# Compressed attention: the upper four token tiles take their exponential without bias and without sum

## The reference, cut to what matters

```python
def compressed_attention(q, k_cmp, v_cmp, pos, slopes):
    end_idx = np.arange(n_cmp) * CMP_STRIDE + CMP_BLOCK - 1
    s = jnp.einsum('bghtd,bgcd->bghtc', q, k_cmp).astype(jnp.float32) * NSA_HEAD_DIM ** -0.5
    dist = (pos[:, :, None] - pos[:, end_idx][:, None, :]).astype(jnp.float32)
    valid = np.arange(S)[:, None] >= end_idx[None, :]
    s = s - slopes[None, :, :, None, None] * dist[:, None, None]
    s = jnp.where(valid, s, NEG_INF)
    m = jnp.max(s, axis=-1, keepdims=True)
    p = jnp.where(valid, jnp.exp(s - m), 0.0)
    p = p / jnp.maximum(jnp.sum(p, axis=-1, keepdims=True), 1e-20)
    o = jnp.einsum('bghtc,bgcd->bghtd', p.astype(v_cmp.dtype), v_cmp)
    return o, p
```

## Time and profile before

| what | value |
|---|---|
| median of 3 runs | 2379.27 us (2377.95 to 2382.49) |
| profiled execution | 2378.9 us, span in the profile 2377.1 us |
| busy over the span | PE 89%, DVE 40%, ACT 30%, POOL 20% |
| the stage | from 1329 us to the barrier, next matmul at 1416.75 us |

### The profile page before, as it was taken

How to read it: one execution, slowest core, us unless ns; L and a number is a source line. 1 busy time by engine, 2 the same in 40 slices (tenths; PEclk the granted TensorE clock), 3 DMA queues, 4 the chain that set the end, 5 groups by cost and what they waited for, 6 DMA issues and landing times. The chain is left out here.

```text
span 2377.1 us, 32726 instructions
## 1 busy us (share of the span) xinstructions
PE 2119.5 (89%) x12669; PEld 1469.5 (62%) x12669; DVE 960.4 (40%) x2286; ACT 717.8 (30%) x1775; POOL 474.0 (20%) x617
## 2 busy tenths in 40 slices
PE   6997759999899999967999648999999999999995
PEld 3444336655688888843654525666665568888883
DVE  3997864532512111113123576666662242111111
ACT  3014455511111111130121656676662111111110
POOL 0001003321112222100000334454441001222211
PEclk9998769999899999989999779999999998999998
DMA  5000011031779999954000100001002147999995
GB/s 204 0 0 0 0 62 37 19 101 71 298 270 358 366 368 368 325 171 106 0 1 0 74 1 10 11 20 45 10 10 74 62 173 275 360 366 370 369 349 137
DMA packets 88034, 347.27 MB, mean 146 GB/s; under 512 B 16721, under 2 KB 21864, under 8 KB 70919
## 3 DMA queue, kind: packets, MB, share of 16 engines
q1 hardware_dynamic: 69446, 278.03, 30.4%
q0 software_dynamic: 18432, 67.12, 10.9%
HBM read 288.84 MB, written 60.47 MB: 147 GB/s over the span
## 5 line engine op out<-in xcount | busy, mean ns | idle before, releaser
L1530 PEld LDWEIGHTS experts_gu_ps<-experts_x_cols,moew_gate 128*128 128x128 f32 x2048 | 242.3, 195 | 34.3 <-issue 34.3
L1530 PE MATMUL experts_gu_ps<-experts_x_cols,moew_gate 128*128 128x128 f32 x2048 | 243.2, 278 | 4.6 <-DVE experts_x_cols L1567 4.6
L1530 PE MATMUL experts_gu_ps<-experts_x_cols,moew_up 128*128 128x128 f32 x2048 | 239.1, 275 | 0.0
L1530 PEld LDWEIGHTS experts_gu_ps<-experts_x_cols,moew_up 128*128 128x128 f32 x2048 | 233.8, 192 | 0.0
L1541 PE MATMUL experts_y_ps<-moew_down,experts_hid 128*128 128x512 f32 x512 | 230.5, 593 | 2.0 <-DVE trunk_x_rows L1623 2.0
L1070 POOL TENSOR_SCALAR nsaatt_probs<-nsaatt_probs,nsaatt_inv,trunk_gates_or_logits 128x384 f32<-128x384 f32 (+7 forms) x256 | 181.6, 726 | 209.3 <-DVE nsaatt_inv L1095 209.3
L1616 DVE TENSOR_TENSOR experts_sig<-experts_gu_ps,experts_sig 128x256 f32<-128x256 f32 x64 | 27.2, 425 | 440.3 <-ACT experts_sig L1579 440.3
L1041 ACT ACTIVATE nsaatt_probs<-nsaatt_probs,nsaatt_bias 128x384 f32<-128x384 f32 (+7 forms) x256 | 169.0, 667 | 17.7 <-DVE nsaatt_bias L1090 17.7
L1470 POOL DMA_INDIRECT x_kept<-trunk_x_rows,moe_index x64 | 101.4, 1585 | 308.0 <-DVE trunk_x_rows L1623 214.0
L1541 PEld LDWEIGHTS experts_y_ps<-moew_down,experts_hid 128*128 128x128 f32 x512 | 92.5, 191 | 95.4 <-issue 95.4
L1579 ACT ACTIVATE experts_sig<-experts_gu_ps 128x256 f32<-128x256 f32 x64 | 24.7, 386 | 416.6 <-PE experts_gu_ps L1530 416.6
(11 more groups left out here) (377 smaller groups left out, 3229.1 us busy)
## 6 DMA issues: line engine op xcount, KB each, us to landing
moew_gate<-in_moe_w_gate_dram SPq DMA_DIRECT2D x64, 1024.0 KB, 7.5
moew_up<-in_moe_w_up_dram SPq DMA_DIRECT2D x64, 1024.0 KB, 11.8
moew_down<-in_moe_w_down_dram SPq DMA_DIRECT2D x64, 1024.0 KB, 15.1
trunk_x_rows<-in_x_dram SPq DMA_DIRECT2D x16, 512.0 KB, 4.7
x_kept<-trunk_x_rows SPq DMA_DIRECT2D x16, 512.0 KB, 2.6
h_rows<-out_h_rows SPq DMA_DIRECT2D x16, 512.0 KB, 2.6
trunk_x_rows<-x_kept SPq DMA_DIRECT2D x16, 512.0 KB, 4.1
l0b_w_in<-in_mix_w_in_dram SPq DMA_DIRECT2D x1, 5760.0 KB, 23.7
```

The source lines that it names most:

```text
L1530: last = pe.matmul(to, wm[:, c, half * P:(half + 1) * P], x_cols[:, s % 2, c, :], start=(c == 0), stop=(c == CHUNKS - 1))
```

## The change

For the upper four tiles (`BY_ROW` = 4 to 7) the exponential takes neither a bias nor a sum. DVE subtracts the row's maximum in `e` itself, in one instruction of 4 tiles by 2 heads by 63 keys (504 elements), placed in `shift(i)` between the maximum and the bias. ACT then takes four tiles of one head in one activation of 252 elements, so a pair has two such activations and eight of the old kind, ten in place of sixteen (`EXPS`). The sums of the upper tiles are a reduction of 504 elements at the head of `normalise(i)` on DVE. It waits only for the two wide activations, which ACT takes first. `shifted` now counts two for a pair, and ACT waits for both.

```diff
+    BY_ROW = TILES // 2
+    EXPS = 2 * BY_ROW + 2
+    REST = (P, TILES - BY_ROW, 2, W)
...
                 def exps(i):
-                    act.wait_ge(shifted, i + 1)
+                    act.wait_ge(shifted, 2 * (i + 1))
                     if i >= 2:
                         act.wait_ge(p_ready, i - 1)
-                    for t in range(TILES):
+                    for h in range(2):
+                        rows = e[:, i % 2, BY_ROW:, h, 0:W]
+                        act.activation(rows, rows, ACT.Exp, scale=SLOPES[2 * i + h]).then_inc(exped, 1)
+                    for t in range(BY_ROW):
                         for h in range(2):
                             act.activation(e[:, i % 2, t, h, 0:W], ... bias=..., accum_out=...).then_inc(exped, 1)
...
                     mine.link(dve.tensor_reduce(top[:, :, :], rows, X_AXIS, ALU.max))
+                    dve.tensor_tensor(rows[:, BY_ROW:], rows[:, BY_ROW:], over(top[:, BY_ROW:, :].unsqueeze(3), REST),
+                                      ALU.subtract).then_inc(shifted, 1)
                     if i >= 2:
-                        dve.wait_ge(exped, 2 * TILES * (i - 1))
-                    dve.tensor_tensor(bias[:, b], top[:, :, :], over(slopes[:, 2 * i:2 * i + 2, 1].unsqueeze(1), (P, TILES, 2)),
-                                      ALU.mult).then_inc(shifted, 1)
+                        dve.wait_ge(exped, EXPS * (i - 1))
+                    dve.tensor_tensor(bias[:, b, 0:BY_ROW], top[:, 0:BY_ROW, :],
+                                      over(slopes[:, 2 * i:2 * i + 2, 1].unsqueeze(1), (P, BY_ROW, 2)), ALU.mult).then_inc(shifted, 1)
...
                 def normalise(i):
...
-                    dve.wait_ge(exped, 2 * TILES * (i + 1))
+                    dve.wait_ge(exped, EXPS * i + 2)
+                    dve.tensor_reduce(total[:, b, BY_ROW:, :], rows[:, BY_ROW:], X_AXIS, ALU.add).then_inc(rest_summed, 1)
+                    dve.wait_ge(exped, EXPS * (i + 1))
+                    dve.wait_ge(rest_summed, i + 1)
```

More of the change, by code:

```diff
@@ L2348, in compressed @@
                                 "added", "turned", "copied", "valued", "out_ready"))
-        gates_ready = ph.sem("gates_ready")
+        gates_ready, rest_summed = ph.sem("gates_ready"), ph.sem("rest_summed")
         with nc.Block() as block:
```

## The result

The changed kernel takes 2385.53 us (median of 10 runs, 2384.39 to 2390.57), the kernel before 2379.93 us in the same series (10 runs, 2377.5 to 2382.49): 5.6 us more. Over all the runs, not from the two medians, the ratio is 1.0026 with a 95% interval of 1.0016 to 1.0036. It is slower, by a little more than a measurement of this kernel can tell from no change. The forecast was 2385.1 us, from a median before of 2379.27; its sum was 5.9 us more.

The account below looks back on a forecast made before the run. The prediction took a DVE-POOL loop of 6.82 us a turn, not ACT, as the bound. Start -1.13, turns +6.55 and end +0.5 gave +5.9 us, predicted 2385.1 us, range 2381.9 to 2387.4 (8 in 10).

Parts of the forecast that it names:

- What bounds the stage: Stage of the change: DVE's waits for POOL's product close each 6.82 us turn; ACT, at 98%, stands beside.
- The two DVE instructions: Subtraction in shift 0.60 us, reduction in normalise 0.71 us; together 1.31 us a pair, bounds 1.20 to 1.45.
- What ACT saves: Six activations fewer a pair, 3.4 us of exponentials in place of 5.3; worth 0 in the repeating turns.
- the ring: Loop of DVE's shift and normalise, then POOL's product, then the next shift: a turn from 6.82 to 8.13 us, +6.55 altogether.
- The start: First shift to the mask of pair 0: the mask comes 1.13 us sooner.
- The end: Last pair: ACT's 3.50 us wait goes without gain, DVE's operations meet busy POOL; +0.5 us, bounds -1.0 to +1.3.
- The subtraction beside POOL's additions: In each turn the subtraction meets only the additions' end: 0 to 0.15 us for each of five pairs, taken as 0.
- Behind the stage: The next stage starts behind a barrier with nothing in flight, so the stage's whole delay is handed on.
- A: Last pair's product runs freely, giving back 1.0 us, and the instructions cost 1.20 a pair: +3.9, 2383.2 us; chance 26%.
- B: Every subtraction sits out an addition's tail (0.15 x 5) and the last pair costs +1.3: +7.5, 2386.8 us; chance 16%.
- C: DVE's idle 1.82 us a turn absorbs the new work and ACT was the bound: -2.4, 2376.9 us; chance 5%.
- D: The wide activation costs as much as four narrow ones, 1.33 us: +8, 2387.3 us; chance 3%.

Follow-up runs that it names:

- third buffer: Three e buffers in place of two: on the changed kernel 2386.68 us (ratio 1.0030 to the kernel before), on the kernel before 2378.90 us (0.9997).
- early sum: Changed kernel with the reduction of pair i + 1 moved behind p of pair i: 2382.94 us, ratio 1.0013 to the kernel before.
- the halves: Changed kernel cut to DVE's subtraction alone, 2383.17 us (ratio 1.0013 to the kernel before), or to DVE's sum alone, 2383.48 us (1.0015).

## Why the prediction was right, point by point

- *What bounds the stage.* Right, and shown: the waits of 1.82 us stand in the changed kernel as before, they vanish with a third buffer, and the sum moved into them is free.
- *The two DVE instructions.* 0.60 for the subtraction as forecast, 0.77 for the reduction in place of 0.71; a pair costs 1.36 us in place of 1.31, within the bounds of 1.20 to 1.45. Both durations (0.68, 0.67) were right; the 0.06 more lie between the reduction's end and the mask (0.10 us, where 0.03 was taken), which now waits for two semaphores. With the early sum the mask has the same two waits, long met, and follows the bias as closely as ever, 0.08 us from start to start; so the second wait costs nothing when it is met in advance. What makes the 0.06 here was not tested by itself.
- *What ACT saves.* Nothing in the ring, as forecast. The wide activation took 0.40 us, 0.31 from start to start, not 0.49 and 0.40: it carries neither bias nor sum, unlike the row from which it was taken. It changed no sum, since DVE was the later of the two. Two wide ones and the first narrow one behind them:

```profile
1335.91 0.72 ACT L2418 ACTIVATE cmpatt_e<-cmpatt_e 128x252 f32<-128x252 f32 x2 [4.05 <-DVE cmpatt_bias L2464]
1336.54 0.33 ACT L2421 ACTIVATE cmpatt_e<-cmpatt_e,cmpatt_bias 128x63 f32<-128x63 f32 x1
```

- *The start.* -1.10 for -1.13.
- *The end.* +0.27 for +0.5. The mechanism was the one described, with mask, clamp and weight held in turn; POOL's product came 10.81 us after shift(7), where 11.1 was forecast. The size was less than the +0.5 to +1.3 for which the exclusion of DVE and POOL was said to speak: of the 0.27, 0.06 is POOL's order of work, as forecast (10.60 in place of 10.54), and only 0.21 the holding.
- *The subtraction beside POOL's additions.* Nothing, as forecast: 0.68 us in every turn. It was a near thing: the additions end 0.01 us before the subtraction starts (1346.45 and 1346.46). The third buffer shows what it costs when it comes earlier.
- *Behind the stage.* Handed on, as far as the spread of the rest lets one say: 5.98 us of stage stand beside 5.6 us between the medians, and beside 6.5 us between the two spans, in which the part behind the stage happens to be 0.9 us longer and the part ahead 0.3 us shorter.
- *The sum.* That it came within 0.1 us of the stage's 5.98 is in part luck: the pairs cost 0.26 more than forecast, the end 0.23 less.
- *The rivals.* The argument against A (the product at 1008 elements is near its own rate) was false: it takes 1.87 us alone. It didn't come true because p is written beside the last product as well. B's price was not reached. C is refuted by the halves and the third buffer; its arithmetic on ACT was sound (ACT's 7.2 us a pair are 0.4 more than the ring's 6.82), but its conclusion was not. D is refuted by the wide activation's 0.40 us.

## What to carry to other kernels

An engine at 98% in a stage need not bound it: look which wait closes a turn, and price an added instruction by whether it stands between that wait's end and the next engine's start, or within the idle time itself. The same reduction cost 0.77 us in one place and nothing some 5 us earlier in the same queue. Where DVE and POOL both read SBUF, freeing DVE from a semaphore can turn the wait into a longer instruction; so compare the durations of identical instructions in the two traces, and not only the lists of waits.

## What the runs showed of the hardware

- A DVE operation with two inputs in SBUF, even of 8 elements a partition, waited for POOL's running instruction: 1.22 us for 0.16 (third buffer, changed kernel). The clamp, one input and 16 elements, did so too: 0.80 for 0.17 (the changed kernel's end). The maximum and the add from PSUM did not: 1.20 and 1.20 us beside POOL in the third-buffer kernel, as elsewhere.
- POOL is held in the same way: its product of 1008 elements took 1.87 us with p written before it, but 2.77 with DVE's p started 0.16 us ahead of it.
- A 63-element activation with either a bias per partition or a sum followed its predecessor at 0.24 us (the two halves of the change); with both at 0.33.
